# Five reordered joints in a two-layer hybrid DiT block on one core, with the first modulation weights in four pairs

## Chip, cores and metric

One NeuronCore of a Trainium2 chip. The metric is device time in microseconds (us) of one execution; the lower the better.

## The reference

Two layers over 512 latent tokens and 256 context tokens of width 1024, in fp32. Each layer modulates an RMS-normed input with factors that come from a conditioning vector through `w_mod`, projects it with `w_in`, runs four mixers side by side (global attention, windowed attention with a sink, gated linear attention "GLA", mLSTM), projects with `w_out`, and adds a squared-ReLU MLP:

```python
for l in range(DEPTH):
    mod = s_c @ w_mod[l] + b_mod[l]; mod_c = s_cc @ w_mod[l] + b_mod[l]
    ...
    h = rms_norm(x, g_norm1) * (1.0 + sc1) + sh1          # context: xc, mod_c
    z = split(h @ w_in)
    o_a, o_b, o_c, o_d = global_gqa(z), window_gqa(z), gla(z), mlstm(z)
    x = x + ga1 * (concat(o_a, o_b, o_c, o_d) @ w_out)
    h = rms_norm(x, g_norm2) * (1.0 + sc2) + sh2
    x = x + ga2 * (square(relu(h @ w_mlp1)) @ w_mlp2)     # context only in layer 0
```

## The kernel before

It is written in raw Bass: every engine has its own instruction list, and semaphores join them. SyncE (SP) issues nearly all transfers, so a transfer also waits for those ahead of it in SP's list.

**Weights.** A weight slot is 1024x256 numbers, 1 MB, held as a 128x2048 tile. Every fp32 product is made of three passes: high part of the weight by high part of h, the same by the low part of h, low part of the weight by the high part of h. So a slot goes the way: load into `raw[0]` (`load_w`, which waits for `lo_ready` of the slot before, as there is one such buffer), ScalarE (ACT) rounds it to `w_hi` (L808, 128x2048), and a subtraction gives `w_lo`. In the input and output projections this is done by GpSimd (POOL; `low`, L703, four pieces of 128x512); in layer 0's MLP by VectorE (DVE; `low_w`, L2045). `w_hi` and `w_lo` have two buffers each.

**Start.** The tiles of x and context are transposed on TensorE (PE) and copied by ACT (L834); ACT squares them (L842), DVE adds the squares (L1459), PE sums over partitions (L2368). Eight modulation matrices `first_mod` (shift in four, scale in four, 1 MB each) are loaded next and multiplied with the conditioning (L2297); two copies (L1471) and 16 tiny matmuls (L2310, `first_mods_columns`) turn the rows into columns `modall`, and the gain `gs` follows (L1480). Then `norm` runs for k = 0 to 7, a 128-row chunk each: DVE multiplies (L1491), ACT modulates (L908, 512 and 256 columns) and rounds to `h_hi` (L912), DVE subtracts to `h_lo` (L1486), and PE's `feature_pair` multiplies the chunk with slot 0 (L2343).

**Input projection.** Twelve slots s, two halves m. In layer 0 eight more modulation matrices go through one buffer (`raw` number 51, called `raw[1]` in the code): PE sums one at (0,0), (0,1), (1,0), (2,0) to (4,0) (`mod_rows_sum`, L2297); DVE copies the row (`mod_copy`, L1425); PE turns it into columns (`mod_columns`, L2324) ahead of the next half; DVE adds the bias (L1418). The next matrix loads once the sum before is done. Beside the products DVE runs the scans of GLA and mLSTM (L1679, L1717, L1731), ACT their exponentials, POOL the exponents of the GLA levels (L724, L725, L731).

**Other joints.** Entry of layer 0's MLP: `norm_mlp` in two halves of the tokens, then `mlp`, whose first products wait for `w_lo` of the blocks (`mlp_raw`, named "11", "12" and so on). Entry of layer 1 and of its MLP: `norm` and `feature_pair` again, while POOL makes `w_lo` of the first two slots. End: after the last product of the last MLP quarter (`plain_quarter`) PE transposes the result back (L2904), DVE copies it (L2260), SP stores it (L691) in four row blocks.

## Time and profile before

| | |
|---|---|
| median of 3 runs | 1928.3 us (1926.76 to 1931.65) |
| the profiled execution | 1930.06 us, its span 1927.5 us |
| mean granted TensorE clock | 0.964 |
| busy share: PE, DVE, ACT, POOL | 92%, 56%, 39%, 22% |
| POOL's weight differences (L703) | 256 pieces, 346.5 us |

The span runs from the first to the last instruction in the trace; 2.6 us of the execution lie around it. Times in the trace count from the span's start. A row of the timeline gives start, duration, engine, line, operation, what it writes and reads, how many instructions it holds, and in brackets how long the engine was idle before it and what ended that. A release named there is inferred from semaphores.

### The profile page before, as it was taken

The page shows a single profiled execution, that of the slowest core. Times are in us where ns is not written, and L with a number is a line of the kernel's source. Part 1 is how long each engine was busy: PE and PEld are TensorE (multiplying, and loading weights), DVE is VectorE, ACT ScalarE, POOL GpSimd, SP SyncE. Part 2 cuts the span into 40 slices and gives each one's busy share as a digit, 9 for nine tenths or more (in the row PEclk, how much of TensorE's full clock was granted, in tenths as well). Part 3 has the DMA queues.
Part 4 walks back from the last instruction along what each step waited for, and adds up shares of the span by engine and source line. Part 5 has one row for each costly group of instructions (what it writes and reads, how often), then busy time and mean ns, then how long its engine had stood idle before and what let it go on. Part 6 is the DMA issues. An engine that isn't in the chain of part 4 may idle for free.

```text
span 1927.5 us, 27988 instructions
## 1 busy us (share of the span) xinstructions
PE 1772.6 (92%) x11328; PEld 1533.5 (80%) x11328; DVE 1082.3 (56%) x1638; ACT 745.0 (39%) x1026; POOL 430.0 (22%) x316
## 2 busy tenths in 40 slices
PE   6898999988897999999999989999979989999998
PEld 4778897767776999989999868788667768777776
DVE  2373636676626798796987956555666342213132
ACT  3522325643214643534535463234642252323130
POOL 1231632200220000000000033452201334444542
PEclk8899999999998999999999989999898989999999
DMA  7640112100054617547266113221200212222221
GB/s 316 200 156 23 46 65 75 58 1 1 1 196 182 233 67 273 223 150 313 88 253 259 44 69 126 99 77 67 88 1 1 87 66 87 88 108 87 87 88 66
DMA packets 34432, 217.61 MB, mean 113 GB/s; under 512 B 4724, under 2 KB 5146, under 8 KB 15642
## 3 DMA queue, kind: packets, MB, share of 16 engines
...
q14 instruction: 30, 0.25, 0.0%
...
## 4 chain that ended last, share of the span: by engine, by line
PE 72%; DVE 12%; issue 5%; ACT 4%; DMA 3%; POOL 2%; SPq 1%; DVEq 0%; ACTq 0%; POOLq 0%
PE ps L2356 24%; PE ps L2788 20%; PE ps L2533 8%; PE ps L2343 2%; DMA raw<-w_big 2%; PE ps L2613 2%; POOL w_lo L703 2%; PE ps L2728 1%; DMA raw<-w_modl 1%; DVE xT L2085 1%; PE ps L2659 1%; DVE mx L1798 1%; PE ps L2666 1%; PE ps L2461 1%; PE ps L2297 1%
## 5 line engine op out<-in xcount | busy, mean ns | idle before, releaser
L703 POOL TENSOR_TENSOR w_lo<-raw,w_hi 128x512 fp32r<-128x512 f32 x256 | 346.5, 1384 | 1179.1 <-ACT w_hi L808 1179.1
L2788 PE MATMUL ps<-op_hi,w_hi 128*128 128x384 f32 x896 | 308.0, 344 | 21.5 <-DVE w_lo L2045 8.7
L2788 PE MATMUL ps<-op_hi,w_lo 128*128 128x384 f32 x896 | 305.1, 340 | 0.0
L2788 PE MATMUL ps<-op_lo,w_hi 128*128 128x384 f32 x896 | 305.1, 340 | 0.0
L808 ACT ACTIVATE w_hi<-raw 128x2048 fp32r<-128x2048 f32 x64 | 122.2, 1910 | 195.3 <-PE ps L2356 131.0
L2788 PEld LDWEIGHTS ps<-op_hi,w_hi 128*128 128x128 f32 x896 | 171.4, 191 | 29.1 <-issue 15.5
L2788 PEld LDWEIGHTS ps<-op_lo,w_hi 128*128 128x128 f32 x896 | 171.2, 191 | 0.0
L2788 PEld LDWEIGHTS ps<-op_hi,w_lo 128*128 128x128 f32 x896 | 171.1, 191 | 0.0
L2356 PE MATMUL ps<-h_hi,w_hi 128*128 128x512 f32 x496 | 166.7, 378 | 0.1
L2356 PE MATMUL ps<-h_lo,w_hi 128*128 128x512 f32 x496 | 161.9, 369 | 0.0
L2356 PE MATMUL ps<-h_hi,w_lo 128*128 128x512 f32 x496 | 161.8, 368 | 0.0
L1940 DVE SCALAR_TENSOR_TENSOR xT<-ps,modall,xT 128x512 f32<-128x512 f32 (+1 forms) x56 | 39.0, 711 | 196.0 <-PE ps L2356 191.3
L1207 ACT ACTIVATE w_hi<-raw 128x1024 fp32r<-128x1024 f32 x80 | 84.6, 1058 | 151.3 <-PE ps L2788 140.2
L2533 PE MATMUL ps<-w_hi,h_hi 128*128 128x256 f32 x448 | 133.1, 297 | 1.0 <-POOL w_lo L703 1.0
L2533 PE MATMUL ps<-w_lo,h_hi 128*128 128x256 f32 x448 | 127.0, 284 | 0.0
L2533 PE MATMUL ps<-w_hi,h_lo 128*128 128x256 f32 x448 | 126.7, 283 | 0.0
L2045 DVE TENSOR_TENSOR w_lo<-raw,w_hi 128x1024 fp32r<-128x1024 f32 x80 | 96.6, 1218 | 18.6 <-ACT w_hi L1207 18.6
L2356 PEld LDWEIGHTS ps<-h_hi,w_hi 128*128 128x128 f32 x496 | 85.7, 192 | 21.8 <-issue 2.7
L2356 PE MATMUL ps<-hid_lo,w_hi 128*128 128x512 f32 x256 | 101.5, 396 | 0.0
L2356 PE MATMUL ps<-hid_hi,w_lo 128*128 128x512 f32 x256 | 101.5, 396 | 0.0
L2356 PE MATMUL ps<-hid_hi,w_hi 128*128 128x512 f32 x256 | 101.5, 396 | 0.0
L2356 PEld LDWEIGHTS ps<-h_hi,w_lo 128*128 128x128 f32 x496 | 85.3, 190 | 16.7
...
## 6 DMA issues: line engine op xcount, KB each, us to landing
raw<-w_big SPq DMA_DIRECT2D x96, 1024.0 KB, 4.8
raw_m<-w_modl SPq DMA_DIRECT2D x20, 1024.0 KB, 6.3
raw<-w_modl SPq DMA_DIRECT2D x16, 1024.0 KB, 5.0
op_hi<-op_cache SPq DMA_DIRECT2D x21, 768.0 KB, 4.7
op_lo<-op_cache SPq DMA_DIRECT2D x21, 768.0 KB, 6.3
first_mod<-w_modl SPq DMA_DIRECT2D x8, 1024.0 KB, 19.0
...
op_cache<-op_hi SPq DMA_DIRECT2D x7, 768.0 KB, 3.3
```

What stands on the lines that cost most here:

```text
L703: ins = nc.gpsimd.tensor_tensor(w_lo[r][:, ks, :], raw[raw_r][:, ks, :], w_hi[r][:, ks, :].bitcast(F32), ALU.subtract)
L808: nc.scalar.activation(w_hi[w % 2][:], raw[raw_of(w)][:], ACT.Copy).then_inc(sem("hi_ready"), 1)
L1207: nc.scalar.activation(chunk(w_hi[r], c_), src, ACT.Copy).then_inc(sem("mw_hi"), 1)
L1798: step(v.tensor_reduce(mx[:, u % 2, hb:hb + 1], bank(2 * hb, lo, T - lo), AX_X, ALU.max, negate=True))
L1940: ins = v.scalar_tensor_tensor(xT[:, k, a:b], pair(k, a, b - a), mt[:, ga + k, c_i:c_i + 1], xT[:, k, a:b], ALU.mult, ALU.add)
L2045: v.tensor_tensor(chunk(w_lo[r], c_), src, chunk(w_hi[r], c_).bitcast(F32), ALU.subtract).then_inc(sem("mw_lo"), 1)
L2085: ins = v.scalar_tensor_tensor(xT[:, k, t0:t1_], bank(b, t0 - th * h, t1_ - t0), mt[:, 40 + k, c_i:c_i + 1], xT[:, k, t0:t1_], ALU.mult, A ...
L2343: ins = mm(pair(g + m, a, b - a), w[:, k, m * P:(m + 1) * P], mov[hl][:, k, a:b], start=(k == 0 and q == 0), stop=(k == KD - 1 and q == 2))
L2356: ins = mm(pair(g, a, b - a), w[:, k, m * P:(m + 1) * P], mov[hl][:, k, a:b], start=(k == 0 and q == 0), stop=(k == KD - 1 and q == 2))
L2533: ins = mm(pair(g, (j - j0) * 256, 256), (h_hi, h_lo)[hl][:, k, cols(j)], w[:, k, :], start=(k == 0 and q == 0), stop=(k == KD - 1 and q = ...
L2613: ins = mm(ps[64 * hb:64 * hb + 64, 7 * 512 + p * P:7 * 512 + p * P + P], v_ab[:, kt, m * P + 64 * hb:m * P + 64 * hb + 64], probT[u % 2][ ...
L2788: ins = mm(bank(base + g, 0, h), wide(w)[:, k, g * P:(g + 1) * P], ops[hl][:, k, 0:h], start=(p in FRESH and k == 0 and q == 0), stop=(k = ...
```

## The change

1. **Start.** SP loads slot 0's weight ahead of the modulation matrices, and these as four pairs (shift and scale of the same two chunks). ACT squares each x tile straight from PSUM (a second ACTIVATE per tile), DVE sums it per tile (`tile_sum`, one TENSOR_REDUCE), `w_lo` of slot 0 is made by DVE (`low_w0`). Rows, columns and gain are made pair by pair: the first two pairs ahead of the products, the third and fourth among the products of `feature_pair` (ahead of k = 2 and 3, and 4 and 5); the row of the modulation at (0,0) is summed ahead of k = 6, the one at (0,1) after the pair.
2. **Differences on DVE.** In both input projections DVE subtracts `w_lo` of slot s+1 as its first instruction of slot s, in one 128x2048 piece; POOL keeps the GLA exponents.
3. **MLP entry.** In layer 0 the last output modulation goes to another buffer, block "12" is loaded right behind it, its high parts are made ahead of the second half's chunks, and the columns are turned after product 0.
4. **Entries of layer 1 and of its MLP.** POOL starts the difference of the second slot only when six chunks of h are done.
5. **Output.** PE transposes each chunk one group after its products, ACT copies in three parts, SP stores three column parts; the last copy is shared with DVE.

`OUT_PARTS` is ((0, 4), (4, 7), (7, 8)).

```diff
-    for j in range(FIRST_MODS):
-        sp.dma_start(first_mod[j][:], mslot(j)).then_inc(slot_landed(j), 16)
+    load_w(wslot(0), 0)
+    for i in range(FIRST_MODS // 2):
+        for j in (i, FIRST_MODS // 2 + i):
+            sp.dma_start(first_mod[j][:], mslot(j)).then_inc(slot_landed(j), 16)
+    load_w(wslot(1), 1)
+    load_mod(mslot(FIRST_MODS))
+    sp.wait_ge(sem("x_trans"), 2)
-    load_w(wslot(0), 0)
-    load_mod(mslot(FIRST_MODS))
-    load_w(wslot(1), 1)
...
-        for k in range(4, OUT_MODS[0]):
+        for k in range(4, OUT_MODS[0] - 1):
+        load_mod(mslot(out_mod(l, OUT_MODS[0] - 1)), raw_m)
+        load_block("12", 0, 0)
-        load_block("12", 0, 0)
...
-    for j in range(LAT_TILES):
-        sp.wait_ge(sem("out_ready"), j + 1)
-        sp.dma_start(out[cols(j), :], xout[j % 2][:]).then_inc(sem(f"out_stored{j % 2}"), 16)
-    for r in range(2):
-        sp.wait_ge(sem(f"out_stored{r}"), 16 * (LAT_TILES // 2))
+    for (done, n), (k0, k1) in zip((("out_ready", 4), ("out_ready", 8), ("out_last", 2)), OUT_PARTS):
+        sp.wait_ge(sem(done), n)
+        sp.dma_start(out.rearrange("(j p) c -> p j c", p=P)[:, :, k0 * P:k1 * P],
+                     xout[:, :, k0 * P:k1 * P]).then_inc(sem("out_stored"), 16)
+    sp.wait_ge(sem("out_stored"), 16 * len(OUT_PARTS))
...
     def in_proj(l):
-        for s in range(IN_SLOTS):
-            w = l * PROJ + s + 2
-            for q in range(4 * s, 4 * s + 3):
-                gla_step(l, q)
-            low(w + 1, w % 2)
-            gla_step(l, 4 * s + 3)
+        for q in range(4 * IN_SLOTS):
+            gla_step(l, q)
...
     for l in range(DEPTH):
-        lows(l * PROJ, l * PROJ + 2)
+        if l == 1:
+            low(l * PROJ + 1, 0)
+            gp.wait_ge(sem("h_ready"), KD + 6)
+        low(l * PROJ + 2, 1)
+        gp.wait_ge(sem("lo_ready"), l * PROJ + IN_SLOTS + 2)
-    lows(MLP_1, N_W)
+    low(MLP_1 + 1, 0, raw_of(MLP_1))
+    gp.wait_ge(sem("h_ready"), 2 * KD + 6)
+    low(MLP_1 + 2, 1, raw_of(MLP_1 + 1))
+    lows(MLP_1 + 2, N_W)
...
+        if j >= 2:
+            act.wait_ge(sem("acc_added"), j - 1)
+        nc.scalar.activation(sqx[j % 2][:], pair(j).rearrange("p (k t) -> p k t", k=KD),
+                             ACT.Square).then_inc(sem("sq_ready"), 1)
-        act.wait_ge(sem("x_done"), x_total - KD + k + 1) if x_total else act.wait_ge(sem("x_in"), TILES)
+        act.wait_ge(sem("x_done"), x_total - KD + k + 1)
...
+        high_w(1, 1)
...
-        if l == 0 and which == 1:
-            split_hi(1)
+            if l == 0 and which == 1 and k == 5:
+                split_hi(1)
...
         for P_ in range(PHASES):
-            if P_ + 1 < PHASES or not last:
+            if not (first and P_ == 0) and (P_ + 1 < PHASES or not last):
...
+    def tile_sum(j):
+        dve.wait_ge(sem("sq_ready"), j + 1)
+        v.tensor_reduce(tmp[4][:, cols(j)], sqx[j % 2][:].rearrange("p k t -> p t k"), AX_X,
+                        ALU.add).then_inc(sem("acc_added"), 1)
+    def low_w0():
+        dve.wait_ge(sem("hi_ready"), 1)
+        v.tensor_tensor(w_lo[0][:], raw[0][:], w_hi[0][:].bitcast(F32), ALU.subtract).then_inc(sem("lo_ready"), 1)
...
-        if l == 0 and which == 1:
-            for r in range(2):
-                dve.wait_ge(sem("mod_used"), FIRST_MODS // 2 * (r + 1))
-                v.tensor_copy(mod_rows[:, r * 1024:(r + 1) * 1024],
-                              ps[:, r * 1024:(r + 1) * 1024]).then_inc(sem("mod_rows_ready"), 1)
-            dve.wait_ge(sem("mod_cols"), 1)
-            v.tensor_tensor(modt[0][:, 0:4 * FIRST_MODS].rearrange("p (m c) -> p m c", c=2),
-                            bank(6, 0, 4 * FIRST_MODS).rearrange("p (m c) -> p m c", c=2),
-                            bc(lvec(0, LV_BMOD, 2 * FIRST_MODS), 2), ALU.add).then_inc(sem("mod_out"), 1)
-        dve.wait_ge(sem("mod_out"), mod_n.at(1))
-        nc_ = 2 if which == 1 else 1
-        step(v.scalar_tensor_tensor(gs[:, :, 0:nc_], mt[:, m0:m0 + KD, 0:nc_], 1.0,
-                                    bc(lvec(l, LV_G1 if which == 1 else LV_G2, KD), nc_), ALU.add, ALU.mult))
+        first = l == 0 and which == 1
+        def first_rows(j):
+            dve.wait_ge(sem("mod_used"), 2 * j + 2)
+            v.tensor_copy(mod_rows[:, j % 2 * 512:j % 2 * 512 + 512], bank(7)).then_inc(sem("mod_rows_ready"), 1)
+        def first_gain(j):
+            dve.wait_ge(sem("mod_cols"), j + 1)
+            for m in (2 * j, FIRST_MODS + 2 * j):
+                ins = v.tensor_tensor(mt[:, m:m + 2, :], bank(6, 2 * m, 4).rearrange("p (m c) -> p m c", c=2),
+                                      bc(lvec(0, LV_BMOD + m, 2), 2), ALU.add)
+            step(ins)
+            ins = v.scalar_tensor_tensor(gs[:, 2 * j:2 * j + 2, :], mt[:, m0 + 2 * j:m0 + 2 * j + 2, :], 1.0,
+                                         bc(lvec(0, LV_G1 + 2 * j, 2), 2), ALU.add, ALU.mult)
+            if j == KD // 2 - 1:
+                ins.then_inc(sem("mod_out"), 1)
+                dve.wait_ge(sem("mod_out"), 1)
+            else:
+                step(ins)
+        if first:
+            first_rows(0)
+            low_w0()
+            first_gain(0)
+        else:
+            dve.wait_ge(sem("mod_out"), mod_n.at(1))
+            nc_ = 2 if which == 1 else 1
+            step(v.scalar_tensor_tensor(gs[:, :, 0:nc_], mt[:, m0:m0 + KD, 0:nc_], 1.0,
+                                        bc(lvec(l, LV_G1 if which == 1 else LV_G2, KD), nc_), ALU.add, ALU.mult))
...
         for k in range(KD):
+            ahead = first and k > 0 and k % 2 == 0
+            if ahead:
+                low(k - 1)
+                first_gain(k // 2)
-            if k == 0 and l == 0 and which == 1:
-                make_masks()
-            if k >= 1:
+            if first and k % 2 == 0 and k < KD - 2:
+                first_rows(k // 2 + 1)
+            if k >= 1 and not ahead:
+        if first:
+            make_masks()
+    def low(w):
+        dve.wait_ge(sem("hi_ready"), w + 1)
+        dve.wait_ge(sem("lo_ready"), w)
+        v.tensor_tensor(w_lo[w % 2][:], raw[0][:], w_hi[w % 2][:].bitcast(F32),
+                        ALU.subtract).then_inc(sem("lo_ready"), 1)
         for s in range(IN_SLOTS):
+            if s >= 1:
+                low(l * PROJ + s + 1)
...
-                    if s == 0:
-                        mod_copy(bank(7, 256 * (1 - m), WC), 2 - m)
-                    else:
-                        mod_copy()
+                    mod_copy()
...
+        low(l * PROJ + IN_SLOTS + 1)
...
+                low_w(1, 0)
+                low_w(1, 1)
...
-    def feature_pair(g, r, mov, n_ts, ready, second_mod=False):
+    def feature_pair(g, r, mov, n_ts, ready, with_mods=False):
         for k in range(KD):
-            if second_mod and k == KD // 2:
-                pe.wait_ge(sem("mod_landed"), mods.at(2) * 16)
-                mod_rows_of(7 * 512, raw[1]).then_inc(sem("mod_summed"), 1)
+            if with_mods and k in (2, 4):
+                first_rows(k // 2 + 1)
+            elif with_mods and k in (3, 5):
+                first_columns(k // 2 + 1)
+            elif with_mods and k == 6:
+                mod_rows_sum()
...
-                                 in_mod(l, 0, 1) is not None)
+                                 l == 0)
...
-    def plain_quarter(n_t):
+    def turn_x(k, done):
+        pe.wait_ge(sem("x_done"), done)
+        if k == 4:
+            pe.wait_ge(sem("out_ready"), 4)
+        for j in range(LAT_TILES):
+            to = bank(1 + 2 * (j // 2), j % 2 * P, P) if k == KD - 1 else bank(4 + j, k % 4 * P, P)
+            ins = nc.tensor.transpose(to, xT[:, k, cols(j)], ident)
+        if k in (3, 6, 7):
+            ins.then_inc(sem("x_trans"), 1)
+    def plain_quarter(n_t, last=False):
...
+                    if last and g > 2 * QW1:
+                        turn_x(g - 2 * QW1 - 1, T_("xd").n - 1)
+        if last:
+            turn_x(KD - 1, T_("xd").n)
...
+            if first and (P_, c_) == (0, 0):
+                mod_columns()
...
-            first_mods(0, 4)
-            norm_sum(T)
-            first_mods(4, FIRST_MODS)
-            first_mods_columns()
+            first_rows(0)
+            first_columns(0)
+            norm_sum(T, tmp[4], TILES)
+            first_rows(1)
+            first_columns(1)
...
-            mod_rows_sum()
-            mod_columns()
+            mod_rows_sum(src=raw_m)
```

The order on DVE at the start, from the first copy of modulation rows (`mod_rows`) to the third chunk; `tmp<-xT` is the multiplication of a chunk. Before:

```order
L1471 COPY mod_rows<-ps 128x1024 x2
L1474 TENSOR_TENSOR modall<-ps,vcol_66 128x32
L1480 SCALAR_TENSOR_TENSOR gs<-modall,vcol_66 128x16
L1491 TENSOR_TENSOR tmp_113<-xT,tmp_116 128x768
L1397 CAST lmask<-cload 128x1024
L1398 CAST ident_b<-cst 128x128
L1399 TENSOR_SCALAR m_left<-cload 128x128
L1400 TENSOR_SCALAR m_right<-cload 128x128
L1401 TENSOR_SCALAR p_after<-cload 128x128
L1402 TENSOR_SCALAR p_before<-cload 128x128
L1491 TENSOR_TENSOR tmp_114<-xT,tmp_116 128x768
L1486 TENSOR_TENSOR h_lo<-tmp_117,h_hi 128x768
```

and in the changed kernel:

```order
L1505 COPY mod_rows<-ps 128x512
L1483 TENSOR_TENSOR w_lo_54<-raw_50,w_hi_52 128x2048
L1511 TENSOR_TENSOR modall<-ps,vcol_66 128x4 x2
L1514 SCALAR_TENSOR_TENSOR gs<-modall,vcol_66 128x4
L1544 TENSOR_TENSOR tmp_114<-xT,tmp_117 128x768
L1505 COPY mod_rows<-ps 128x512
L1544 TENSOR_TENSOR tmp_115<-xT,tmp_117 128x768
L1535 TENSOR_TENSOR h_lo<-tmp_118,h_hi 128x768
L1535 TENSOR_TENSOR h_lo<-tmp_119,h_hi 128x768
L1511 TENSOR_TENSOR modall<-ps,vcol_66 128x4 x2
L1514 SCALAR_TENSOR_TENSOR gs<-modall,vcol_66 128x4
L1544 TENSOR_TENSOR tmp_114<-xT,tmp_117 128x768
```

Copies and gains, once in one block ahead of the chunks, now lie among them: the copy of a pair's rows stands between the multiplications of two chunks, its gain ahead of the next two.

The order on PE behind `feature_pair`, where slot 1 begins (`raw_51` is the buffer of the modulation matrices, `mod_part` the copied row). Before:

```order
L2343 MATMUL ps<-h_hi,w_lo_54 128x512
L2343 MATMUL ps<-h_hi,w_lo_54 128x256
L2324 MATMUL ps<-cst,mod_part 128x2 x4
L2297 MATMUL ps<-raw_51,csw 32x256 x8
L2356 MATMUL ps<-h_hi,w_hi_53 128x512
```

and in the changed kernel:

```order
L2417 MATMUL ps<-h_hi,w_lo_54 128x256
L2395 MATMUL ps<-cst,mod_part 128x2 x2
L2363 MATMUL ps<-raw_51,csw 32x256 x8
L2395 MATMUL ps<-cst,mod_part 128x2 x2
L2363 MATMUL ps<-raw_51,csw 32x256 x8
L2430 MATMUL ps<-h_hi,w_hi_53 128x512
L2430 MATMUL ps<-h_hi,w_hi_53 128x256
```

Two modulation matrices from the one buffer are now multiplied between slot 0 and slot 1, where one was.

The order on DVE in slots 2 and 3 of layer 0 (`vc` is a copy of the values, `pre`, `ls` and `bb` belong to GLA's decay and its scans). Before:

```order
L1425 COPY mod_part<-ps 128x256
L1540 COPY vc<-ps 128x1024
L1552 SCALAR_TENSOR_TENSOR ls_178<-pre_176 128x768
L1418 TENSOR_TENSOR modall<-ps,vcol_66 128x4
L1425 COPY mod_part<-ps 128x256
L1552 SCALAR_TENSOR_TENSOR ls_179<-pre_177 128x768
L1540 COPY vc<-ps 128x512
L1557 SCALAR_TENSOR_TENSOR pre_176<-pre_176,ls_178 128x768
L1679 SCALAR_TENSOR_TENSOR bb_186<-ones,pre_176 128x128 x6
L1418 TENSOR_TENSOR modall<-ps,vcol_66 128x4
```

and in the changed kernel:

```order
L1559 TENSOR_TENSOR w_lo_55<-raw_50,w_hi_53 128x2048
L1439 TENSOR_TENSOR modall<-ps,vcol_66 128x4
L1446 COPY mod_part<-ps 128x256
L1602 COPY vc<-ps 128x1024
L1614 SCALAR_TENSOR_TENSOR ls_179<-pre_177 128x768
L1439 TENSOR_TENSOR modall<-ps,vcol_66 128x4
L1446 COPY mod_part<-ps 128x256
L1614 SCALAR_TENSOR_TENSOR ls_180<-pre_178 128x768
L1602 COPY vc<-ps 128x512
L1619 SCALAR_TENSOR_TENSOR pre_177<-pre_177,ls_179 128x768
L1741 SCALAR_TENSOR_TENSOR bb_187<-ones,pre_177 128x128 x6
L1559 TENSOR_TENSOR w_lo_54<-raw_50,w_hi_52 128x2048
```

The differences that slots 3 and 4 need (`w_lo_55`, then `w_lo_54`) now stand in DVE's order, each ahead of the bias and the copy of a modulation row, and ahead of the second scan.

## Rows read from the trace of the kernel before

**Rows 1.** Waits of PE over the whole span, grouped by what ended them.

```profile
PE ps L2343 <- DVE h_lo L1486: 17.2, 4, 6.5
PE ps L2324 <- DVE mod_part L1425: 16.5, 4, 6.0
```

**Rows 2.** Timeline of the start, all engines.

```profile
16.46 1.96 ACT L834 ACTIVATE xT<-ps 128x1024 f32<-128x1024 f32 x2 [0.31 <-PE ps L2288]
...
22.62 1.07 PE L2297 MATMUL ps<-first_mod,csw 128*32 128x256 f32 x16 [1.43 <-DMA first_mod<-w_modl]
...
25.11 1.93 PE L2297 MATMUL ps<-first_mod,csw 128*32 128x256 f32 x16 [1.41 <-DMA first_mod<-w_modl]
...
28.31 2.07 PE L2368 MATMUL ps<-tmp,ones 128*128 128x512 f32 x2 [1.27 <-DVE tmp L1459]
...
38.02 6.99 PE L2310 MATMUL ps<-cst,mod_rows 128*128 128x2 f32 x32 [1.35 <-DVE mod_rows L1471]
39.63 1.91 ACT L808 ACTIVATE w_hi<-raw 128x2048 fp32r<-128x2048 f32 x1 [6.58 <-DMA raw<-w_big]
...
50.94 0.98 PE L2343 MATMUL ps<-h_hi,w_hi 128*128 128x512 f32 x2 [4.06 <-DVE h_lo L1486]
```

**Rows 3.** The same timeline, one chunk of the cycle.

```profile
60.17 1.29 ACT L908 ACTIVATE tmp<-tmp,modall,gs 128x512 f32<-128x512 f32 x2
60.21 0.51 PE L2343 MATMUL ps<-h_hi,w_hi 128*128 128x512 f32 x2
60.30 0.96 DVE L1486 TENSOR_TENSOR h_lo<-tmp,h_hi 128x768 fp32r<-128x768 f32 x1 [0.25 <-ACT h_hi L912]
...
61.49 0.84 ACT L912 ACTIVATE h_hi<-tmp 128x768 fp32r<-128x768 f32 x1
```

**Rows 4.** The page's table of the costliest groups, one row (mean ns).

```profile
L2045 DVE TENSOR_TENSOR w_lo<-raw,w_hi 128x1024 fp32r<-128x1024 f32 x80 | 96.6, 1218 | 18.6 <-ACT w_hi L1207 18.6
```

**Rows 5.** The page's table of transfers (KB each, us from issue to landing).

```profile
raw<-w_modl SPq DMA_DIRECT2D x16, 1024.0 KB, 5.0
...
op_cache<-op_hi SPq DMA_DIRECT2D x7, 768.0 KB, 3.3
```

**Rows 6.** Timeline of PE, slots 1 to 4 of layer 0.

```profile
71.46 0.50 PE L2324 MATMUL ps<-cst,mod_part 128*128 128x2 f32 x4
...
73.09 1.07 PE L2297 MATMUL ps<-raw,csw 128*32 128x256 f32 x16
...
151.58 1.02 PE L2324 MATMUL ps<-cst,mod_part 128*128 128x2 f32 x4 [6.00 <-DVE mod_part L1425]
```

**Rows 7.** Timeline of PE at the entry of layer 0's MLP.

```profile
603.87 1.01 PE L2324 MATMUL ps<-cst,mod_part 128*128 128x2 f32 x4 [5.99 <-DVE mod_part L1425]
...
634.44 0.42 PE L2788 MATMUL ps<-op_hi,w_hi 128*128 128x384 f32 x1 [3.40 <-DVE w_lo L2045]
```

**Rows 8.** Timeline at the entry of layer 1.

```profile
1126.02 7.18 POOL L703 TENSOR_TENSOR w_lo<-raw,w_hi 128x512 fp32r<-128x512 f32 x4 [6.84 <-ACT w_hi L808]
1127.22 2.90 DVE L1491 TENSOR_TENSOR tmp<-xT,tmp 128x768 f32<-128x768 f32 x2 [3.96 <-ACT tmp L850]
...
1132.21 0.76 PE L2343 MATMUL ps<-h_hi,w_hi 128*128 128x512 f32 x1 [6.27 <-DVE h_lo L1486]
```

**Rows 9.** Timelines of DVE, ACT and POOL in layer 1's input projection.

```profile
1179.46 5.17 DVE L1679 TENSOR_TENSOR_SCAN bb<-ones,pre 128x128 f32<-128x128 f32 x6
...
1186.57 2.00 DVE L1679 TENSOR_TENSOR_SCAN bb<-ones,pre 128x128 f32<-128x128 f32 x6
...
1243.87 0.63 ACT L939 ACTIVATE eqk<-eqk 128x512 f32<-128x512 f32 x1 [5.73 <-POOL eqk L725]
...
1249.14 3.56 POOL L731 TENSOR_TENSOR eqk<-ft,eqk 128x512 f32<-128x512 f32 x1 [0.79 <-ACT eqk L939]
```

**Rows 10.** Timeline of the end.

```profile
1916.64 1.97 PE L2904 MATMUL ps<-cst,xT 128*128 128x128 f32 x16 [0.84 <-DVE xT L1940]
...
1917.77 2.36 DVE L2260 COPY xout<-ps 128x1024 f32<-128x1024 f32 x2 [1.19 <-PE ps L2904]
```

More of the change, by code:

```diff
@@ L1294, in _ @@
                 if l == 0:
-                    for k in range(KD):
-                        square(k, T, 0)
-                norm(l, 1, T, x_total, split=0 if l == 0 else None)
+                    T_("acc").add(TILES)
+                    split_hi(0)
+                norm(l, 1, T, x_total)
                 in_proj(l)
@@ L1419, in mod_out, with mod_copy @@
                                 bc(b, 2), ALU.add).then_inc(sem("mod_out"), 1)
[L1421 to L1423 removed]
+            def mod_copy(src=bank(7, 256, WC)):
+                dve.wait_ge(sem("mod_summed"), sum_n.at(1))
                 dve.wait_ge(sem("mod_used"), sum_n.at(FIRST_MODS))
@@ L2135, in mlp_quarter @@
                     after = P_ + 1 if P_ + 1 < PHASES or not last else None
+                    if first and P_ == 0:
+                        after = None
                     if P_ >= 1:
@@ L2190, in _ @@
                 if l == 0:
-                    for k in range(KD):
-                        add_square(k, T)
+                    for j in range(TILES):
+                        tile_sum(j)
+                    T_("sq").add(TILES)
+                    T_("acc").add(TILES)
                 norm(l, 1, T)
@@ L2254, in _ @@
                 T_("xd").n = xd.n
-            for j in range(LAT_TILES):
-                dve.wait_ge(sem("x_trans"), TILES + j + 1)
-                if j >= 2:
-                    dve.wait_ge(sem(f"out_stored{j % 2}"), 16 * (j // 2))
-                v.tensor_copy(xout[j % 2][:], pair(j)).then_inc(sem("out_ready"), 1)
+            dve.wait_ge(sem("x_trans"), TILES + 3)
+            v.tensor_copy(xout[:, 2:4, 7 * P:8 * P], bank(3, 0, 2 * P).rearrange("p (j c) -> p j c", j=2)).then_inc(
+                sem("out_last"), 1)
         @blk.tensor
@@ L2512, in in_proj @@
                             mod_columns()
-                        if has_mod and (s, m) != (0, 1):
+                        if has_mod and (s, m) != (0, 0):
                             mod_rows_sum()
@@ L2897, in _ @@
                 T_("xd").n = xd.n
-            pe.wait_ge(sem("x_done"), T_("xd").n)
-            for j in range(LAT_TILES):
-                if j >= 2:
-                    pe.wait_ge(sem("out_ready"), j - 1)
-                for k in range(KD):
-                    ins = nc.tensor.transpose(pair(j, k * P, P), xT[:, k, cols(j)], ident)
-                ins.then_inc(sem("x_trans"), 1)
 def _slots(w, widths=WC):
```

54 lines of the change are left out of this document (33 added, 21 removed).

## Prediction

> **What bounds the kernel.** I read the page first, its busy shares and chain: PE is busy nine tenths of the span and owns most of the chain, so only PE's idle time and its half-clock stretches can be won. Next the waits of PE over the span [rows 1]: two kinds matter for this change, 17.2 us in four waits for the first h_lo at an entry, and 16.5 us in four waits of the modulation columns for `mod_part`. Then the timeline of each joint. At the start [rows 2] the reader should see a string: x copied, rows, sums, sixteen columns that take 7 us, and only then the chunks; the first product stands at 50.94. In [rows 6, 7] the columns of a modulation wait for DVE, which is late because of its own list. In [rows 8, 9] DVE's instructions stretch while POOL subtracts. At the end [rows 10] nothing covers the transposes and copies. About 0.3% (5.8 us) is what a measurement of this kernel can tell from no change.
>
> **1. Start.** Prices first. Two ACT copies of an x tile take 1.96 [rows 2], so 12 ACTIVATEs in place of six add about 5.9 us of ACT, of which 1.5 fits into gaps in which ACT waited for PE (one of 0.31 is in the row [rows 2]): the last copy ends near 22.8, where it ended at 18.4. Slot 0's rounding (1.91) [rows 2] brings it to 24.7. DVE's difference of 128x2048 is not in the trace: 1024 columns take 1.22 [rows 4], so twice that, 2.44, is the upper bound, one piece with its fixed part once, about 2.2, the lower; I take 2.3. `w_lo` is there at 27.0. On PE the first pair's rows follow x at 23.9, four columns cost 4 x 0.44 = 1.75 (a quarter of 6.99), the sum over partitions 2.07 plus half of it for the other 256 columns: 29.8. Two ACTIVATEs of the size of a rounding (0.84) [rows 3] give the norm at 31.6, DVE multiplies (0.96) to 32.6, ACT modulates and rounds (1.29 + 0.84) to 34.8, DVE subtracts: **first product at 35.8 instead of 50.94**, 15 us sooner. Transfers allow it: a matrix lands every 2.49 us (22.62 to 25.11) [rows 2].
>
> But the chunks then don't run at their old pace. A chunk was bound by ACT, 1.29 + 0.84 = 2.13. PE needs 6 x 0.35 = 2.1 (pairs of matmuls start 0.35 apart; the one of 0.51 overlaps the next) [rows 3]. In the new order on DVE the copy of a pair's rows stands ahead of the next multiplication, and PE makes these rows only behind the odd chunk's products: DVE waits for PE, PE for the h_lo behind it. One round of two chunks: gain 1.1, multiplication 0.96, ACT 2.13, with PE's two products 4.2, rows 1.07 and four columns 1.0 partly between: I count 8.9 for it, against 4.3. From 35.8: chunk 2 at 43.7, chunk 4 at 52.6, chunk 6 at 60.9, slot 0 done at **65**. POOL's difference of slot 1 falls into chunks 5 to 7 (about 0.5 to 1 on each DVE instruction beside it, as in [rows 8]: +2.5), and PE idles about 2.6 in each round. What idling does to the clock is seen in [rows 2]: after 4.06 idle the pair took 0.98, at the lower level (1.2 GHz), against 0.51 in [rows 3]. If every second round is at that level, +2. I take 69.5 for the end of slot 0, where it was 71.46 [rows 6]; bounds 65 and 76.
>
> Behind slot 0 two matrices now pass through the one buffer instead of one: columns, sum (1.07), then a load that can only begin when that sum is done (5.0) [rows 5], then the next sum: slot 1 starts about 8.1 after slot 0, at 77.6, where it was 74.2 (73.09 + 1.07) [rows 6]: **+3.4**. In slot 3 DVE's list puts the difference for slot 4 ahead of the copy of the modulation row. Its load stands on SP behind a matrix that waits for the sum at the slot's first half; three megabytes at 2.5 each, rounding 1.9, difference 2.3 and the copy are 12 us against a half slot of about 8: PE waits +5 (bounds 0 and 5.6). In return DVE's scans run without POOL beside them: of the 6.00 at 151.58 I take 2.5 back, and of the 4.5 that the total of 16.5 leaves for the two waits not shown [rows 1, 6, 7], 3.9. Layer 0 up to there: 3.4 + 5 - 3.9 - 2.5 = **+2.0**, bounds -8 and +14.
>
> **2. Differences in layer 1's projection.** Twelve per layer, 2.3 each, go to DVE, whose share was a little over half: room in total, not at every place. Won: six scans took 5.17 beside POOL and 2.00 without [rows 9], and ACT once stood 5.73 for POOL's exponents, which were queued behind POOL's difference. Upper bound of the gain 5.7, of the loss two differences on the path, 4.6. Nearer the gain, as nothing on SP waits for PE here: **-3.0**.
>
> **3. MLP entry.** The columns that waited 5.99 [rows 7] go behind product 0. Next late is the chain of chunks on DVE and ACT, which gets two 128x1024 differences (2.44) put in front: 5.99 - 2.44 = **-3.6**, with bounds 0 (the chain is as late as before) and -9.4 (the 3.40 goes too).
>
> **4. Layer 1's two entries.** Beside POOL two multiplications took 2.90, alone 1.92 (0.96 each) [rows 3], and the h_lo behind them is stretched alike: at most 1.7 ahead of the first product at 1132.21 [rows 8]; **-1.4** there and **-1.5** at the MLP's entry, whose wait is the longest of the four, 6.5 [rows 1]. Lower bound nothing, if the later difference makes slot 1 late. The Trainium skill's page "SBUF — State Buffer", section "SBUF: two separate sides", calls the port pair of the two engines "an exclusive lock, not a bandwidth split": the loser blocks for the whole instruction. By it three instructions would each lose up to a POOL piece, 1.8, and the entry would win up to 5.4. The row shows half a microsecond for each, so it bears out a partial stretch only.
>
> **5. Output.** Sixteen transposes take 1.97 [rows 10], four 0.49; six groups of four move in among the products, +2.95 there. Behind the last product: 0.5, four ACT copies of 128x384 (by 2.36 for two of 1024 columns, 0.5 each) 2.0, a transfer of 768 KB (3.3) [rows 5], some 0.8 of issue: 9.55 in all, where 11.7 passed from 1915.8 to the end at 1927.5: **-2.2**, bounds 0 and -3.5.
>
> **Sum.** 2.0 - 3.0 - 3.6 - 1.4 - 1.5 - 2.2 = -9.7. From the profiled execution, 1930.1, to 1920.4; that execution lies 1.8 above the median of the runs, so I forecast **1919**, with 1913 to 1925 as this case's own range.
>
> **Rivals.** *The start pays in full*: no half clock and no stretch, slot 0 ends at 65, slot 1 at 73, the wait in slot 3 is absorbed by the lead: layer 0 wins 6 instead of losing 2, and layer 1 the full 5.7: 1919 - 8 - 2.7, **1908**. For it: transfers and w_lo are early. Against: the round on DVE and PE, which the order shows.
>
> *DVE blocked behind its new first instruction* (slower): in layer 0 the weight's load waits on SP for a sum of PE, DVE waits for the weight, PE's columns wait for DVE's copy. I priced it in one slot; if the ring closes in each of slots 1 to 4, 5 us each, that is 15 more, and with slot 0 at 76 another 6: 1919 + 21, **1940**. It decides where the difference ends later than a half slot, some 8 us, after the first half's sum. For it: the queue order on SP and 5.0 per load. Against: most loads have a slot of lead.
>
> *The waits change hands*: POOL's exponents wait for DVE's 2.3 us pieces as DVE waited for POOL's. An exponent of POOL took 3.56 beside DVE work [rows 9]. Then 2 and 4 win nothing, and 3 is taken by the chain: 1919 + 9.5, **1928**, no change. The lock that the page above states is this rival's rule; the trace bears it out in that one row.
>
> **Chances.** Forecast 0.5, full start 0.16, ring 0.17, hands 0.17. Faster by over 0.3% means under 1922.5: full start and 0.34 of the forecast, 0.50. Slower means over 1934.1: the ring and a little of the bounds at the start, 0.18. Between: 0.32. The range goes from 1907, the full start, to 1936, short of the ring.
>
> **What would show it.** Right: first product near 36, rounds of about 9, some of them at the lower clock; slot 0 done near 69.5, slot 1 at 77 to 78; a new wait of PE for `mod_part` in slot 3; no POOL difference inside the projections; the entry of layer 0's MLP without its 5.99; some 9.5 from the last product but for the transposes. Wrong: rounds of 4 to 5 (the full start), waits for `mod_part` in several slots (the ring), or POOL's exponents above 3 us throughout (hands).

## The result, and the profile after

The changed kernel took **1932.5 us** (median of 20 runs, 1927.9 to 1938.7), the kernel before **1926.8** in the runs beside it (20 runs, 1922.2 to 1931.7): ratio **1.0036**, 95% interval 1.0028 to 1.0044. It is slower, where 1919 and faster was forecast. The two profiled executions lie closer together (1930.06 before, 1931.35 after) than the medians, so places are read from the traces and totals from the runs.

To see where the time went I matched the products in both traces, the nth of a source line with the nth of the same line, and took the difference of their starts, called the lag below. Positive is later than in the kernel before; the left column is the time in the trace of before. The columns other than "changed" are runs that the next section explains.

| place (us in before) | changed | start_only | diffs_only | gate_only | only_mlp_out | early_rows | best1_late |
|---|---|---|---|---|---|---|---|
| first product (50.9) | -15.6 | -14.2 | -0.9 | -0.9 | -0.3 | -17.3 | -13.9 |
| slot 1, first product (74.1) | +9.7 | +10.0 | -0.1 | -0.3 | -0.6 | -8.6 | -8.3 |
| slot 2, first product (85.8) | +9.5 | +9.9 | -1.9 | -1.4 | 0.0 | -9.3 | -9.5 |
| slot 3, second half (120.1) | +14.9 | +8.4 | +3.8 | -2.9 | -1.5 | -3.5 | -11.0 |
| scans done (209) | +8.1 | +8.7 | -3.1 | -2.5 | -2.0 | -9.2 | -15.2 |
| output projection (505) | +8.4 | +11.5 | +0.8 | -2.6 | -2.6 | -5.3 | -15.0 |
| MLP under way (725) | +2.6 | +11.1 | -2.0 | -3.1 | -7.1 | -11.3 | -22.1 |
| layer 1, before its entry (1118) | +2.9 | +11.5 | -2.1 | -3.1 | -7.1 | -11.3 | -22.1 |
| layer 1, end of the pair (1148) | +1.6 | +11.3 | -2.2 | -4.3 | -7.0 | -12.4 | -22.2 |
| layer 1, slot 2 under way (1160.9) | +6.0 | +11.3 | -2.2 | +4.6 | -7.0 | -7.7 | -22.2 |
| layer 1, late in the projection (1325) | +7.4 | +11.7 | -0.8 | +4.7 | -6.7 | -6.4 | -20.7 |
| last product (1915.4) | +6.7 | +8.7 | -1.6 | +4.4 | -7.2 | -5.9 | -20.4 |

The zero of this table is one execution, and it moves by some 2 to 3 us: gate_only and only_mlp_out have the kernel before's layer 0 up to its MLP, and still read -2.0 to -2.5 at 209. The profiled execution of before lies 3.3 above the median of its 20 runs.

The first product came as forecast, at 35.36 for 35.8; its lead was gone within the slot. PE's timeline of the changed kernel (start, duration, line, operation, how many; in brackets its idle time before and what ended it; L2417 is the pair's product, L2363 the rows of a modulation matrix):

```profile
35.36 0.59 PE L2417 MATMUL ps<-h_hi,w_hi 128*128 128x512 f32 x2 [1.65 <-DVE h_lo L1535]
...
41.28 1.93 PE L2363 MATMUL ps<-first_mod,csw 128*32 128x256 f32 x32
...
45.76 0.62 PE L2417 MATMUL ps<-h_hi,w_hi 128*128 128x512 f32 x2 [2.55 <-DVE h_lo L1535]
...
57.09 1.01 PE L2417 MATMUL ps<-h_hi,w_hi 128*128 128x512 f32 x2 [2.55 <-DVE h_lo L1535]
...
68.12 1.01 PE L2417 MATMUL ps<-h_hi,w_hi 128*128 128x512 f32 x2 [3.29 <-DVE h_lo L1535]
...
81.94 1.93 PE L2363 MATMUL ps<-raw,csw 128*32 128x256 f32 x16 [4.27 <-DMA raw<-w_modl]
```

and DVE's timeline of the same kernel (L1505 is the copy of a pair's rows, L1544 the multiplication, L1535 the h_lo):

```profile
43.28 0.69 DVE L1505 COPY mod_rows<-ps 128x512 f32<-128x512 f32 x1 [4.67 <-PE ps L2363]
43.89 0.95 DVE L1544 TENSOR_TENSOR tmp<-xT,tmp 128x768 f32<-128x768 f32 x1
44.76 0.95 DVE L1535 TENSOR_TENSOR h_lo<-tmp,h_hi 128x768 fp32r<-128x768 f32 x1
```

The pairs of chunks begin at 35.36, 45.76, 57.09 and 68.12: rounds of 10.4 to 11.3 us. In the first, DVE stands 4.67 before the copy (2.67 in the second, at 54.61), for rows that PE makes behind the odd chunk, and PE then stands 2.55 for the h_lo behind that copy. The third round has no copy: its gain waits 2.31 for columns that stand behind a chunk of PE, two multiplications of DVE take 3.96 beside POOL's difference, where two alone take 1.92, and PE stands 3.29. At 81.94 PE waits for the second of two matrices through one buffer. The windows show what the idling does to the clock; first the stretch from the first product to slot 0's end in the kernel before, then the same stretch in the changed kernel (length, busy us of PE, its weight loads, DVE, ACT, POOL, granted clock, share of DMA, GB/s):

```profile
51.00:71.50 20.50, 19.88 (x114) 16.71 (x114) 12.05 (x14) 15.81 (x22) 5.04 (x4) 0.90 0.62 122
```

```profile
34.00:75.00 41.00, 31.26 (x192) 24.71 (x193) 19.89 (x32) 17.66 (x24) 5.73 (x4) 0.79 0.32 120
```

A granted clock of 0.79 is a mixture of the two levels, 2.4 and 1.2 GHz; [rows 2] and the x2 rows above show them apart, 0.98 to 1.01 for the pair against 0.59 to 0.62.

In slot 3 PE waits, as forecast, for a copy that stands behind the new difference (timelines of DVE and PE, L2395 the columns). The last row is slot 4's, which answers to the wait of 6.00 in [rows 6]:

```profile
129.39 2.29 DVE L1559 TENSOR_TENSOR w_lo<-raw,w_hi 128x2048 fp32r<-128x2048 f32 x1 [8.78 <-ACT w_hi L816]
...
131.67 0.41 DVE L1446 COPY mod_part<-ps 128x256 f32<-128x256 f32 x1
...
132.14 1.02 PE L2395 MATMUL ps<-cst,mod_part 128*128 128x2 f32 x4 [5.30 <-DVE mod_part L1446]
...
162.06 1.01 PE L2395 MATMUL ps<-cst,mod_part 128*128 128x2 f32 x4 [5.03 <-DVE mod_part L1446]
```

The entry of layer 0's MLP answers to [rows 7]. The wait for the columns ahead of product 0 is gone, and product 0 starts with a lag of 1.3 where the places before it had 6.2. A wait of product 1 is gone too, which neither the rows nor the prediction list; in the kernel before it was

```profile
620.18 0.69 PE L2788 MATMUL ps<-op_hi,w_hi 128*128 128x384 f32 x1 [5.34 <-DVE w_lo L2045]
```

Product 2 then waits 11.34 in the changed kernel, where it waited 3.40, and at 646 the lag is 2.1:

```profile
606.05 0.44 PE L2877 MATMUL ps<-op_hi,w_hi 128*128 128x384 f32 x1 [1.73 <-DVE op_lo L2054]
636.29 0.66 PE L2877 MATMUL ps<-op_hi,w_hi 128*128 128x384 f32 x1 [11.34 <-DVE hid L2141]
```

In layer 1's projection the weight chain of slot 2 is late. Timelines of SP, ACT, DVE and PE of the changed kernel (loads of `w_big` are weight slots):

```profile
1151.63 0.33 SPq L494 DMA_DIRECT2D raw<-w_big  x1
...
1157.91 1.92 ACT L816 ACTIVATE w_hi<-raw 128x2048 fp32r<-128x2048 f32 x1 [5.78 <-DMA raw<-w_big]
...
1159.92 2.29 DVE L1559 TENSOR_TENSOR w_lo<-raw,w_hi 128x2048 fp32r<-128x2048 f32 x1 [9.51 <-ACT w_hi L816]
...
1162.26 0.39 PE L2607 MATMUL ps<-w_hi,h_hi 128*128 128x256 f32 x1 [2.01 <-DVE w_lo L1559]
...
1216.07 2.28 DVE L1559 TENSOR_TENSOR w_lo<-raw,w_hi 128x2048 fp32r<-128x2048 f32 x1
...
1224.63 1.22 DVE L1455 SCALAR_TENSOR_TENSOR raw<-raw 128x1024 f32<-128x1024 f32 x1 [5.62 <-DMA raw<-w_modl]
...
1227.77 1.51 PE L2455 MATMUL ps<-cst,r 128*128 128x128 f32 x6 [3.36 <-DVE snap L1704]
```

In the kernel before, POOL's difference of that entry is not held back, and the load was issued 18 us earlier:

```profile
1133.22 0.33 SPq L492 DMA_DIRECT2D raw<-w_big  x1
```

The last three rows of the longer block show the other half. The difference at 1216.07 stands behind DVE's scans, so the buffer comes free late. The row of a modulation matrix that SP loads behind the next weight then lands late, and DVE waits 5.62 for it ahead of the snapshots.

The end answers to [rows 10] (L2828 transposes, L1342 copies, L696 the transfers):

```profile
1922.36 0.60 PE L2828 MATMUL ps<-cst,xT 128*128 128x128 f32 x4
1922.99 1.64 ACT L1342 ACTIVATE xout<-ps 128x384 f32<-128x384 f32 x4 [16.11 <-PE ps L2828]
...
1924.66 0.94 SPq L696 DMA_DIRECT2D out<-xout  x2
```

The last matched product is 6.7 late and the span's end 2.1 (1929.6 against 1927.5): 4.6 is won behind the products, and 2.6 of it was spent on transposes among them.

### The profile page after: what moved, and what is told of

Its sections match the earlier page's. It is cut to its first block, busy times and chain, and to the rows that moved or that the text cites. A ratio compares the mean times of both kernels' runs of the same rounds, so it can differ in the third digit from the quotient of the medians.

```text
span 1929.6 us, 27933 instructions
## 1 busy us (share of the span) xinstructions
PE 1767.8 (92%) x11328; PEld 1531.9 (79%) x11328; DVE 1113.4 (58%) x1671; ACT 747.5 (39%) x1033; POOL 296.0 (15%) x216
## 4 chain that ended last, share of the span: by engine, by line
PE 75%; DVE 12%; ACT 5%; issue 4%; DMA 2%; POOL 1%; DVEq 0%; SPq 0%; ACTq 0%
PE ps L2430 26%; PE ps L2877 19%; PE ps L2607 8%; PE ps L2417 4%; PE ps L2687 2%; PE ps L2363 1%; PE ps L2535 1%; DVE xT L2149 1%; PE ps L2802 1%; DMA raw<-w_modl 1%; DMA raw<-w_big 1%; PE ps L2733 1%; DVE w_lo L2109 1%; DVE mx L1860 1%; PE ps L2740 1%
## 5 line engine op out<-in xcount | busy, mean ns | idle before, releaser
L708 POOL TENSOR_TENSOR w_lo<-raw,w_hi 128x512 fp32r<-128x512 f32 x156 | 209.7, 1375 | 890.6 <-ACT w_hi L816 851.0
L2877 PE MATMUL ps<-op_hi,w_hi 128*128 128x384 f32 x896 | 307.3, 343 | 27.4 <-DVE hid L2141 11.3
L2430 PEld LDWEIGHTS ps<-h_hi,w_lo 128*128 128x128 f32 x496 | 85.8, 192 | 16.6
```

Of the source, the lines that this page charges most:

```text
L708: ins = nc.gpsimd.tensor_tensor(w_lo[r][:, ks, :], raw[raw_r][:, ks, :], w_hi[r][:, ks, :].bitcast(F32), ALU.subtract)
L2430: ins = mm(pair(g, a, b - a), w[:, k, m * P:(m + 1) * P], mov[hl][:, k, a:b], start=(k == 0 and q == 0), stop=(k == KD - 1 and q == 2))
L2877: ins = mm(bank(base + g, 0, h), wide(w)[:, k, g * P:(g + 1) * P], ops[hl][:, k, 0:h], start=(p in FRESH and k == 0 and q == 0), stop=(k = ...
```

## The experiments

Four theories had to be told apart: the start loses; DVE's list of differences loses; the gate at layer 1 loses; or the wins at the MLP's entry and the output are given back. First each part was undone in the changed kernel, or done alone.

**no_start**: part 1 undone, parts 2 to 5 kept (here PE's share of the edit).

```diff
-                    first_rows(0)
-                    first_columns(0)
-                    norm_sum(T, tmp[4], TILES)
-                    first_rows(1)
-                    first_columns(1)
+                    first_mods(0, 4)
+                    norm_sum(T)
+                    first_mods(4, FIRST_MODS)
+                    first_mods_columns()
```

> The changed kernel with part 1 (start in pairs) undone, parts 2 to 5 kept. Theory 'the start loses' (rounds of two chunks at 12 us, then two modulation matrices one after the other through one buffer: PE 9.6 us late at slot 2's first product): that is won back, less the lead with which slot 4's waits shrank: 7 to 9 us below the changed kernel, 1 to 4 below before. Rival 'the start is neutral, the loss is in the projections behind it': as slow as the changed kernel, 5 to 6 above before.

Measured: 1922.3, ratio to before 0.9982 (0.9971 to 0.9993). That is 10 below the changed kernel, a little more than the theory's 7 to 9: the start is the largest loss.

**no_diffs**: part 2 undone; POOL subtracts again.

```diff
-                    if s >= 1:
-                        low(l * PROJ + s + 1)
+                    low(w + 1, w % 2)
```

> The changed kernel with part 2 (differences on DVE) undone: POOL subtracts in both projections, all else kept. Theory 'DVE's list delays the one weight buffer': PE's wait of 5.3 in slot 3 of layer 0 goes, but the scans stretch again there (about even), and in layer 1 the 3.9 that PE lost at the snapshots goes: 2 to 6 us below the changed kernel. Rival 'layer 1 loses by the gate of part 4, not by the differences': layer 1's projection stays 4 to 6 us longer than before, total within 2 us of the changed kernel.

Measured: 1933.6, ratio 1.0040 (1.0027 to 1.0054). The rival held. In this trace the lag rises from -2.4 to +6.2 at slot 2 of layer 1, where PE waits 5.39 for POOL's `w_lo`. The gate costs more without DVE's differences than with them (there +1.6 to +6.0).

**no_gates**: both gates of part 4 taken out.

```diff
-                    gp.wait_ge(sem("h_ready"), KD + 6)
-            gp.wait_ge(sem("h_ready"), 2 * KD + 6)
```

> The changed kernel without part 4's two gates: POOL starts the second difference at once. Theory 'the gate at layer 1 frees the weight buffer 18 us later and slot 2 pays': the entries lose their 1.5 and 1.0, slot 2 starts without its wait of 2.0 and some 4 us sooner: 1 to 3 us below the changed kernel. Rival 'the gates win what they won at the entries': 2.5 us above the changed kernel.

Measured: 1931.4, ratio 1.0022 (1.0011 to 1.0033), by the medians 1.1 below the changed kernel, at the edge of what was expected. The lag of the trace stays at 7.85 from layer 1's entry past slot 2, as the theory has it; in the changed kernel it rises there by 3.1 (2.9 to 6.0).

**only_mlp_out**: parts 3 and 5 alone (one line of each).

```diff
+                high_w(1, 1)
...
+                    turn_x(KD - 1, T_("xd").n)
```

> The kernel before with parts 3 (MLP entry) and 5 (output) alone. Theory 'these two win where the traces say': 3.3 and 2.0 us, 4 to 6 below before. Rival 'what they win is lost to half-clock stretches and later waits': within 2 us of before.

Measured: 1918.2, ratio 0.9964 (0.9950 to 0.9978): 7 to 8 below before, where 4 to 6 was expected. In its trace the lag falls by 3.6 at the MLP's entry (-2.8 to -6.4 at 646) and by 2.0 at the end (-4.6 behind the products, +2.6 among them); both stay won. The rest of the 7 to 8 was not traced to a place.

Then the mechanisms were tried one by one.

**early_rows**: the changed kernel, with PE making the last two pairs' rows and columns earlier, and the sum at (0,0) one chunk earlier, and DVE taking the gains ahead of the h_lo before them. These edits were not tried apart.

```diff
                     first_columns(1)
+                    first_rows(2)
...
-                    if with_mods and k in (2, 4):
-                        first_rows(k // 2 + 1)
-                    elif with_mods and k in (3, 5):
-                        first_columns(k // 2 + 1)
-                    elif with_mods and k == 6:
+                    if with_mods and k in (2, 4):
+                        first_columns(k // 2 + 1)
+                        if k == 2:
+                            first_rows(3)
+                    elif with_mods and k == 5:
                         mod_rows_sum()
...
-                        low(k - 1)
                         first_gain(k // 2)
...
-                    if k >= 1 and not ahead:
+                    if k >= 1:
```

> The changed kernel, only that PE makes the rows of pair 3 behind the columns of pair 2 (ahead of the first chunk), those of pair 4 ahead of chunk 2, the columns of pairs 3 and 4 ahead of chunks 2 and 4, and DVE takes each gain ahead of the h_lo before it. Theory 'DVE's copy waits for rows that stand behind PE's odd chunk, and PE for the h_lo behind that copy': rounds shrink from 11.7 to 6 to 7 us, PE stays at the upper clock level, slot 0 ends near 60 to 62 instead of 75; slot 1 starts 12 to 14 sooner, some of it lost at slot 4's columns: total 6 to 12 below the changed kernel. Rival 'the rounds are long because of the half clock and POOL's difference': slot 0 still ends past 68, total within 3 of the changed kernel.

Measured: **1917.0**, ratio 0.9955 (0.9940 to 0.9970), 15 below the changed kernel, where 6 to 12 was expected. PE's timeline and the windows of this kernel:

```profile
33.65 0.61 PE L2417 MATMUL ps<-h_hi,w_hi 128*128 128x512 f32 x2
...
40.78 0.62 PE L2417 MATMUL ps<-h_hi,w_hi 128*128 128x512 f32 x2
...
45.86 0.60 PE L2417 MATMUL ps<-h_hi,w_hi 128*128 128x512 f32 x2
...
52.31 0.61 PE L2417 MATMUL ps<-h_hi,w_hi 128*128 128x512 f32 x2 [0.84 <-DVE h_lo L1536]
...
63.64 1.94 PE L2363 MATMUL ps<-raw,csw 128*32 128x256 f32 x16 [3.90 <-DMA raw<-w_modl]
```

```profile
33.00:57.00 24.00, 22.92 (x177) 18.02 (x168) 19.66 (x31) 16.83 (x23) 7.92 (x4) 1.00 0.59 220
```

Rounds are 7.1, 5.1 and 6.5 us, the granted clock is 1.00 throughout, PE waits 0.84 once, and slot 0 ends at 56.6, sooner than expected. POOL's difference lies in the same stretch here (7.92 us), so most of the long rounds was the crossing of the two lists and the clock that fell in its gaps; POOL's share can be no more than part of the third round's wait. The wait of 3.90 for the load at slot 1 is still there.

**sum_in_pair**: the changed kernel, with the modulation at (0,1) summed ahead of chunk 7.

```diff
+                    elif with_mods and k == 7:
+                        pe.wait_ge(sem("mod_landed"), mods.at(2) * 16)
+                        mod_rows_of(7 * 512, raw[1]).then_inc(sem("mod_summed"), 1)
...
-                        if has_mod and (s, m) != (0, 0):
+                        if has_mod and (s, m) not in ((0, 0), (0, 1)):
```

> The changed kernel, only that the modulation at (0,1) is summed ahead of chunk 7 in the pair, as the kernel before did ahead of chunk 4, so that the matrix of (1,0) loads before slot 0 ends. Theory 'two matrices one after the other through one buffer': PE's wait of 4.27 at slot 1 goes, and the half clock behind it: slot 1 starts 5 to 7 sooner, total 3 to 7 below the changed kernel. Rival 'slot 1 is bound by something else (its weight, the columns)': slot 1 starts less than 2 sooner.

Measured: 1928.5, ratio 1.0016 (1.0006 to 1.0026), 4 below the changed kernel, as expected. The wait of 4.27 at slot 1 shrank, on PE's timeline:

```profile
76.49 1.07 PE L2367 MATMUL ps<-raw,csw 128*32 128x256 f32 x16 [1.05 <-DMA raw<-w_modl]
```

Slot 1 begins 6.3 sooner than in the changed kernel. Of that, 2.0 was there at the first product, which the edit does not touch, so the places here overstate the edit.

**gate_only**: the kernel before with the gate at layer 1's entry.

```diff
-                lows(l * PROJ, l * PROJ + 2)
+                low(l * PROJ + 1, 0)
+                if l == 1:
+                    gp.wait_ge(sem("h_ready"), KD + 6)
+                low(l * PROJ + 2, 1)
```

> The kernel before with the gate at layer 1's entry alone. Theory 'the gate frees the weight buffer late': the entry wins 1 to 1.5, slot 2 of layer 1 starts 6 to 9 late: total 5 to 7 above before. Rival 'the gate wins what the entry wins, the loss in layer 1 was the differences on DVE': 1 to 1.5 below before.

Measured: 1933.8, ratio **1.0040** (1.0027 to 1.0053). POOL, SP and PE of this kernel:

```profile
1138.58 7.12 POOL L703 TENSOR_TENSOR w_lo<-raw,w_hi 128x512 fp32r<-128x512 f32 x4 [22.53 <-DVE h_lo L1489]
...
1145.72 0.33 SPq L492 DMA_DIRECT2D raw<-w_big  x1
...
1159.90 0.58 PE L2536 MATMUL ps<-w_hi,h_hi 128*128 128x256 f32 x1 [5.56 <-POOL w_lo L703]
```

The entry wins 1.2 (-3.1 to -4.3), slot 2 loses 8.9 (-4.3 to +4.6). The gated difference ends at 1145.7 and the next weight loads only then; it is rounded and subtracted one after the other, and PE waits 5.56. The loss is 8 us against the 5 to 7 expected.

**start_only** and **diffs_only**: the kernel before with part 1 alone, and with part 2 alone.

```diff
+                    first_rows(0)
+                    first_columns(0)
```

> The kernel before with part 1 alone. Theory 'the start is the loss': slot 1 starts 8 to 11 late, of which 2 to 3 come back at slot 4's columns; 6 to 10 us above before. Rival 'the start loses only together with the differences on DVE': within 3 of before.

```diff
+                    if s >= 1:
+                        low(l * PROJ + s + 1)
```

> The kernel before with part 2 alone (differences on DVE in both projections, no gates). Theory 'about even': in layer 0 slot 3 waits 5 to 7 for mod_part and slot 4 gives it back, -1; in layer 1 the snapshots lose 3.9 and the level sums win 5, +1; total within 3 of before. Rival 'DVE's in-order list loses wherever it is': 4 to 6 above before. Rival 'freeing POOL wins as the scans run unstretched': 4 to 6 below.

Measured: start_only 1936.6, ratio **1.0058** (1.0041 to 1.0075), 1.5 above what was expected: its lag stays near 9 behind slot 4, where 2 to 3 were to come back. diffs_only 1925.0, ratio 1.0001 (0.9991 to 1.0011): even as expected, with a wait of 5.32 in slot 3 of layer 0 and what slot 4 gives back for it.

Last, versions that keep what wins. **best1** is part 1 with the edits of early_rows and sum_in_pair, parts 3 and 5, and the gate at layer 1's MLP alone, where the two slots have buffers of their own; **best1_diffs** adds part 2; **best1_late** puts part 2's difference behind the slot's first copy of a modulation row:

```diff
-                    if s >= 1:
-                        low(l * PROJ + s + 1)
...
                                 mod_copy()
+                        if s >= 1 and m == 0:
+                            low(l * PROJ + s + 1)
```

> Parts 1, 3 and 5 and the gate at the MLP of layer 1 alone, with both mends of the start (early rows, sum inside the pair), without differences on DVE and without the gate at layer 1. If the start's lead carries through: 14 to 20 us below before (10 of the start, 7 to 8 of parts 3 and 5, 1 of the gate). If slot 4's columns, which wait for DVE's scans, eat the lead: 8 to 12 below before.

> best1 with part 2 added. Theory 'about even' for part 2: within 3 of best1's time, with PE's wait for mod_part in slot 3 of layer 0 (5 to 8) and shorter ones at slot 4. Rival 'with the start's lead the DVE list has room': 3 to 6 below best1.

> best1 with part 2, but each difference stands behind the slot's first copy of a modulation row instead of ahead of it. Theory 'slot 3 waits for mod_part because the copy stands behind the difference': that wait goes, 2 to 5 below best1_diffs at slot 4. Rival 'the wait moves to the second half or to slot 4's columns, as the scans are late anyway': within 1.5 of best1_diffs.

Measured: best1 **1907.5**, ratio 0.9905 (0.9890 to 0.9919). best1_diffs 1912.9, ratio 0.9932 (0.9915 to 0.9949), 5 above best1 where within 3 was expected. best1_late **1905.7**, ratio 0.9894 (0.9875 to 0.9913), 7 below best1_diffs: more than the theory's 2 to 5. PE's timelines of best1_diffs and of best1_late at the columns of slots 3 and 4:

```profile
113.87 1.01 PE L2396 MATMUL ps<-cst,mod_part 128*128 128x2 f32 x4 [5.26 <-DVE mod_part L1445]
127.31 0.61 PE L2396 MATMUL ps<-cst,mod_part 128*128 128x2 f32 x4 [0.53 <-DVE mod_part L1445]
143.79 0.98 PE L2396 MATMUL ps<-cst,mod_part 128*128 128x2 f32 x4 [5.04 <-DVE mod_part L1445]
```

```profile
126.23 1.01 PE L2396 MATMUL ps<-cst,mod_part 128*128 128x2 f32 x4 [8.58 <-DVE mod_part L1445]
140.51 0.61 PE L2396 MATMUL ps<-cst,mod_part 128*128 128x2 f32 x4 [0.19 <-DVE mod_part L1445]
```

The wait in slot 3 is gone. The two waits of 5.26 and 5.04 became one of 8.58 in slot 4, so the rival is right in part: some of the wait moved there. Even so 6.4 us less lag remain when the scans are done (-15.2 against -8.8), more than the waits differ; behind the wait of 5.26 best1_diffs runs at a granted clock of 0.57 (114 to 121), where best1_late has 1.00 (109 to 117). best1 and best1_late overlap in their intervals; both beat the kernel before and the changed one.

## Why the prediction was wrong, step by step

The forecast was -9.7, and the two traces differ by +2.1. Of the 11.8 between, layer 0 up to 209 took 6.1 and layer 1's projection 8.8; stretches that nobody priced gave some 3 back, and the rest came as forecast within 1 us. Three terms failed: the rounds of the start with slot 1 behind them, the gate at layer 1, and the differences in layer 1.

**First product**: this was right, 35.36 for 35.8.

**Rounds of two chunks**: the mechanism was named and its size missed. The sum came to 69.5 for slot 0's end; rounds were 10.4 to 11.3 and slot 0 ended at 75.0, near the upper bound of 76. The term that failed is "if every second round is at that level, +2". Products ran at the lower level in every round, and within the chunks their starts add up to 23.3, against 16.7 in early_rows, where the granted clock was 1.00: that is 6.6 in place of 2. A second piece was too small: "rows 1.07" is the price of one matrix, but a pair holds two, 32 matmuls that took 1.93 at 41.28 and again at 52.61.

**Slot 1**: the sum had 8.1 from slot 0's end to its first product; it was 8.8 (75.0 to 83.8), as the second matrix's rows ran at the lower level (1.93 for the 1.07 in the sum). Both together put slot 1 at +9.7 where the sum had +3.4, and layer 0 at +8.1 by 209 where it had +2.0, inside the bounds of -8 and +14. start_only, sum_in_pair and early_rows show the cause.

**Slot 3 and slot 4**: these were right in the main. The wait was 5.30 for 5, and from 120.1 to 209 the lag fell by 6.8, where 6.4 was expected. Slot 3 cost more lag than its wait, though (from 8.0 at 97 to 14.9), as PE came out of the wait at the lower level: the four tiny matmuls at 132.14 took 1.02, where those at 71.46 in [rows 6] took 0.50.

**MLP entry**: the number was right, 3.6 expected, and the lag falls by 4.1 from 6.2 (at 585) to 2.1 (at 646). Its make-up was not: the unlisted wait of 5.34 went as well as the 5.99, and the chain of chunks, which was rightly named as next, took 11.34 at product 2. That the two nearly cancel is luck.

**Layer 1's entry and the gate**: this step failed. The entry won 1.3 as forecast (2.9 to 1.6), but "lower bound nothing, if the later difference makes slot 1 late" left out what stands behind the gated difference: the one weight buffer, and SP's next load. gate_only prices the gate at +7.7 net in the trace, and no_diffs shows it again.

**Differences in layer 1**: -3.0 was forecast, and this failed too. In the changed kernel the projection lost 5.8 from the pair's end (1.6 to 7.4), of which 4.4 belongs to the gate and 1.4 to part 2: +3.8 at the snapshots, -5.2 at the level sums, +3.0 behind. The gain was real: PE's wait of 3.61 at 1246.06 is gone, with ACT's 5.73 for POOL's exponents [rows 9]. The sentence "nothing on SP waits for PE here" was beside the point: SP waits for DVE, and DVE's difference waits behind the scans. Alone, part 2 is even.

**Layer 1's MLP entry** won 1.1 for 1.5 (PE's wait fell from 6.5 to 5.4), and the **output** 2.0 for 2.2 (4.6 - 2.6).

Of the rivals, the ring priced slot 3 rightly but did not close in the other slots. The hands did change, and by the lock. Timelines of DVE and POOL of the changed kernel in layer 1, a difference and the exponent beside it, twice:

```profile
1246.98 2.29 DVE L1559 TENSOR_TENSOR w_lo<-raw,w_hi 128x2048 fp32r<-128x2048 f32 x1 [0.65 <-ACT w_hi L816]
1248.54 1.88 POOL L736 TENSOR_TENSOR eqk<-ft,eqk 128x512 f32<-128x512 f32 x1 [19.86 <-ACT eqk L952]
...
1264.31 2.28 DVE L1559 TENSOR_TENSOR w_lo<-raw,w_hi 128x2048 fp32r<-128x2048 f32 x1
1265.64 2.09 POOL L736 TENSOR_TENSOR eqk<-ft,eqk 128x512 f32<-128x512 f32 x1 [1.54 <-ACT eqk L952]
```

Either exponent ends 1.14 to 1.15 behind the end of DVE's difference, and one with no difference beside it took 1.27: it did its work when DVE was done. The 3.56 of [rows 9] ends 1.14 behind a DVE instruction too (1247.80 to 1251.56). In [rows 8] the 2.90 is one multiplication of 0.96 and one of 2.02, so "half a microsecond for each" was a mean and no partial stretch. The rule quoted from the Trainium skill's page "SBUF — State Buffer" (section "SBUF: two separate sides"), that the loser blocks for the whole instruction, agrees with these rows. It cost little here: of the seven exponents in layer 1 three took 1.88 to 2.31, and no wait of PE in that stretch is put down to them.

The time itself lies inside the range of 1907 to 1936, but on the other side of no change, and that it does is no merit of the sum: the rounds of the start, the gate and the differences all erred towards the gain.

Alone the parts give +0.58% (start), +0.01% (differences), +0.40% (gate), -0.36% (MLP entry and output): 0.63 in sum, where the whole gave 0.36. The four intervals together are nearly as wide as that difference, and the gate at layer 1's MLP was not run alone. In the traces the gate's cost at slot 2 is 8.9 alone and 4.4 with DVE's faster subtraction, which would be most of it.
